# Per-token numbers spread over the partitions by two fp32r products instead of one fp32 product, on one Trainium2 core

## What is computed

```python
def rmsnorm(x, g):
    xf = x.astype(jnp.float32)
    y = xf * lax.rsqrt(jnp.mean(xf * xf, axis=-1, keepdims=True) + EPS)   # one number per token
    return (y * g.astype(jnp.float32)).astype(x.dtype)

# mLSTM, per head and chunk of 128 tokens: a term that depends on the column s alone, ic - b
dmat = b[..., :, None] - b[..., None, :] + ic[..., None, :]
dmat = jnp.where(causal, dmat, -jnp.inf)
m_t = jnp.maximum(inter, dmat.max(axis=-1))
sw = jnp.exp(dmat - m_t[..., None]) * jnp.einsum('bhntk,bhnsk->bhnts', qc, kc)

# odd layer: one softmax over the three dilations, a denominator per token and slot
alpha = jax.nn.softmax(jnp.stack(lses, axis=0), axis=0)
y_c = jnp.einsum('gbsh,gbshe->bshe', alpha.astype(x.dtype), jnp.stack(outs, axis=0))
```

## Time and profile before

| | |
|---|---|
| median of 3 runs | 2983.31 us (2982.22 to 2983.63) |
| the profiled execution's own time | 2986.75 us |
| its span | 2985.0 us |
| mean granted TensorE clock | 0.997 |
| TensorE matmul busy | 2949.0 us, 99% |
| VectorE busy | 1478.3 us, 50% |
| ScalarE busy | 675.4 us, 23% |
| GpSimd busy | 2011.0 us, 67% |
| HBM | 91 GB/s over the span |

### The profile page before, as it was taken

One profiled execution on the slowest core, in us unless ns is written; L12 is line 12 of the kernel. 1 busy time (PEld: TensorE's weight loads), 2 busy tenths in 40 slices (PEclk: granted clock), 3 DMA queues, 4 the chain that ended last, 5 costly groups with the idle time before them and its releaser, 6 DMA issues.

```text
span 2985.0 us, 37813 instructions
## 1 busy us (share of the span) xinstructions
PE 2949.0 (99%) x13898; PEld 2406.9 (81%) x13898; DVE 1478.3 (50%) x2524; ACT 675.4 (23%) x1491; POOL 2011.0 (67%) x2042
## 2 busy tenths in 40 slices
PE   8999999999999999999999999999999999999998
PEld 6887777888888888777888888878888888888887
DVE  7778783633324778775543322565321231424542
ACT  3265353200001346345110000000111111211000
POOL 7775546777777777444777777887776556555775
PEclk9999999999999999999999999999999999999999
DMA  4322222333233322122333333333233223222322
GB/s 147 99 92 65 67 68 77 120 100 97 91 95 127 99 85 93 56 64 62 130 98 92 98 95 103 92 94 100 92 98 106 77 80 105 79 85 78 96 95 77
DMA packets 86921, 274.36 MB, mean 92 GB/s; under 512 B 10368, under 2 KB 11008, under 8 KB 86784
## 3 DMA queue, kind: packets, MB, share of 16 engines
q1 hardware_dynamic: 85248, 270.44, 29.2%
q10 hardware_dynamic: 1536, 2.10, 0.3%
HBM read 266.21 MB, written 4.19 MB: 91 GB/s over the span
## 4 chain that ended last, share of the span: by engine, by line
PE 93%; DVE 5%; POOL 0%; issue 0%; ACT 0%; DMA 0%; DVEq 0%; SPq 0%; POOLq 0%
PE PS L507 59%; PE PS L588 15%; PE PS L858 5%; PE PS L866 3%; PE PS L625 1%; PE PS L904 1%; PE PS L916 1%; PE PS L1155 1%; PE PS L945 1%; PE PS L639 1%; PE PS L928 1%; PE PS L651 1%; DVE SMALLS L1822 0%; PE PS L1130 0%; DVE SQ L1854 0%; PE PS L1142 0%
## 5 line engine op out<-in xcount | busy, mean ns | idle before, releaser
L474 POOL TENSOR_TENSOR WL<-RAW,WH 128x512 fp32r<-128x512 f32 (+2 forms) x538 | 804.2, 1495 | 9.8
L466 POOL TENSOR_TENSOR POOL_C<-POOL_C 128x1 f32<-128x1 f32 x538 | 129.3, 240 | 908.7 <-PE PS L507 518.6
L507 PE MATMUL PS<-XNH,WH 128*128 128x512 f32 (+1 forms) x1712 | 673.7, 394 | 0.7 <-POOL WH L467 0.5
L507 PE MATMUL PS<-XNL,WH 128*128 128x512 f32 (+1 forms) x1712 | 666.9, 390 | 0.0
L471 POOL TENSOR_TENSOR WL<-RAW,WH 128x512 fp32r<-128x512 f32 x420 | 578.9, 1378 | 35.0
L467 POOL TENSOR_SCALAR WH<-RAW 128x1024 fp32r<-128x1024 f32 (+3 forms) x538 | 536.7, 998 | 0.5 <-issue 0.5
L507 PE MATMUL PS<-XNH,WL 128*128 128x512 f32 (+1 forms) x1712 | 423.9, 390 | 0.1
L507 PEld LDWEIGHTS PS<-XNH,WH 128*128 128x128 f32 (+1 forms) x1712 | 320.8, 187 | 70.4 <-issue 3.1
L507 PEld LDWEIGHTS PS<-XNH,WL 128*128 128x128 f32 (+1 forms) x1712 | 320.4, 187 | 68.9 <-POOL WL L474 1.0
L507 PEld LDWEIGHTS PS<-XNL,WH 128*128 128x128 f32 (+1 forms) x1712 | 320.8, 187 | 68.2 <-issue 1.9
L588 PE MATMUL PS<-WH,XNH 128*128 128x512 f32 x704 | 279.1, 396 | 0.2
(11 more groups left out here) (390 smaller groups left out, 4480.1 us busy)
## 6 DMA issues: line engine op xcount, KB each, us to landing
RAW<-w_oslot SPq DMA_DIRECT2D x56, 512.0 KB, 3.6
RAW<-w_L0ffn SPq DMA_DIRECT2D x44, 512.0 KB, 3.6
RAW<-w_L1ffn SPq DMA_DIRECT2D x44, 512.0 KB, 3.6
RAW<-w_od SPq DMA_DIRECT2D x32, 512.0 KB, 3.6
RAW<-w_L0G SPq DMA_DIRECT2D x24, 512.0 KB, 3.6
RAW<-w_L1G SPq DMA_DIRECT2D x24, 512.0 KB, 3.6
RAW<-w_epg SPq DMA_DIRECT2D x16, 512.0 KB, 3.6
RAW<-w_eug SPq DMA_DIRECT2D x16, 512.0 KB, 3.5
```

The costliest lines, as they stand in the source:

```text
L466: nc.gpsimd.tensor_tensor(POOL_C[:, 1:2], POOL_C[:, 0:1], POOL_C[:, 0:1], ALU.add)
L474: nc.gpsimd.tensor_tensor(WL[:, half, at_:w], RAW[:, slot, at_:w], WH[:, half, at_:w].bitcast(F32), ALU.subtract).then_inc(S("weights_spli ...
L507: mm = nc.tensor.matmul(bank, w[:, slot, k * cols:(k + 1) * cols], x[:, k0 + k, :], start=first and j == 0 and w is WH and x is hi, stop=l ...
```

## The change

Every diagonal is made twice: once from the high part of the numbers, rounded to fp32r, and once from the low part, the number less its high part. Both stand in a new buffer SPR (128 x 2 x 512, fp32r), and the parts of the numbers in a new small buffer TINYR. The new function `across` multiplies ones, read as fp32r, by the high and by the low diagonal and lets PSUM add the two. VectorE gets `halve` (two small operations) and `diagonals` (two wide operations, or four of half width at the end). ScalarE writes eight copies a tile instead of four, and TensorE waits for eight. The two new buffers take 4096 + 128 bytes a partition ahead of the shared region, whose end moves with them; WS and BS start at 96 K, INV lies in ARG, and OACC starts at 96 K + 128.

```diff
--- before.py
+++ after.py
@@ -41,7 +41,7 @@
 IN_LAYER = dict(
     conv_raw=8, conv_first=8, conv_acc=8, key_silu=4, mqk_ready=8, v_ready=4, mo_ready=4, small_ready=4, small_staged=1, small_turned=1, sq_raw=4,
     ckvq_raw=4, sk_raw=4, sv_ready=4, dq_raw=4, dk_raw=4, dv_ready=4, nab_ready=1, nab_exp=2,
-    ln_ready=1, lf_ready=1, bg_ready=1, bg_taken=1, diag_ready=16, u_ready=1, den_ready=4, ub_ready=4, ub_taken=4, darg_ready=1,
+    ln_ready=1, lf_ready=1, bg_ready=1, bg_taken=1, diag_ready=32, u_ready=1, den_ready=4, ub_ready=4, ub_taken=4, darg_ready=1,
     pex_ready=17, ms_ready=4, sw_ready=4, kt_ready=3, ktm_copied=3, vw_ready=12, cl_ready=3,
     state_ready=3, swt_ready=4, swt_copied=4, n2_ready=3, n2_taken=3, n1_ready=4, tot_ready=4,
     ya_tm=4, tr_ready=29, tr_copied=29, sq_normed=1, sk_normed=1, dq_normed=1, dk_normed=1,
@@ -186,6 +186,8 @@
         RT = sb(ctx, "RT", [P, T])
         TMP = sb(ctx, "TMP", [P, 2, T])
 
+        SPR = sb(ctx, "SPR", [P, 2, T], F32R)
+        TINYR = sb(ctx, "TINYR", [P, 32], F32R)
         SQA = sb(ctx, "SQA", [P, T])
         small = sb(ctx, "SMALLS", [P, 512])
 
@@ -243,6 +245,9 @@
         TOP8 = tiny(8)
         RTOK = tiny(4)
         RSK = tiny(32)
+        UH, UL = TINYR[:, 0:16], TINYR[:, 16:32]
+        RTH, RTL = UH[:, 0:4], UL[:, 0:4]
+        OSH, OSL = RTH, RTL
         OMX, ONEG, OSUM, OXM = ARG[:, 0:8], ARG[:, 8:16], ARG[:, 16:24], ARG[:, 24:32]
 
         DMS = (DM, X[:, 7, :], SQA[:, :], DG)
@@ -309,7 +314,8 @@
                               skip=16 * K)
         (PLL,) = overlay(("PLL", [P, 2, T], F32R), skip=48 * K)
         GA, ET = SQ, TMP
-        WS, BS, INV = overlay(("WS", [P, 4, P]), ("BS", [P, 4, P]), ("INV", [P, 4, 16]), skip=99840)
+        WS, BS = overlay(("WS", [P, 4, P]), ("BS", [P, 4, P]), skip=96 * K)
+        INV = ARG[:, 0:64].rearrange("p (g t) -> p g t", g=4)
 
         OYH, OYL, OQK = overlay(("OYH", [P, 16, T], F32R), ("OYL", [P, 16, T], F32R), ("OQK", [P, 2, 6, T]))
         OS, OPT = overlay(("OS", [P, NT, T]), ("OPT", [P, NT, T]), skip=16 * K)
@@ -319,7 +325,7 @@
         DIST, SLOPE, BIAS = overlay(("DIST", [P, T]), ("SLOPE", [P, 24]), ("BIAS", [P, T]), skip=92 * K)
         OT = TMP
         ODC, OZ = overlay(("ODC", [P, 2, T]), ("OZ", [P, 2, 6, P]), skip=64 * K)
-        (OACC,) = overlay(("OACC", [P, 2, T]), skip=98 * K + 128)
+        (OACC,) = overlay(("OACC", [P, 2, T]), skip=96 * K + 128)
         OGD = TMP
         (XOUT,) = overlay(("XOUT", [P, KD, T]), skip=64 * K)
         (SQ_FIRST,) = overlay(("SQ_FIRST", [P, KD, T]), skip=68 * K)
@@ -432,7 +438,7 @@
                     sp.dma_start(WS[:, :, :], dram["ws"]).then_inc(S("even_consts"), 16)
                     sp.dma_start(BS[:, :, :].rearrange("p g t -> p (g t)"),
                                  dram["bs"].to_broadcast([P, 4 * P])).then_inc(S("even_consts"), 16)
-                    sp.dma_start(INV[:, :, :].rearrange("p g t -> p (g t)"),
+                    sp.dma_start(ARG[:, 0:64],
                                  dram["inv"].to_broadcast([P, 64])).then_inc(S("even_consts"), 16)
                 if name == "eout":
                     sp.wait_ge(S("x_updated"), 8 * 4)
@@ -609,12 +615,18 @@
                 mm.then_inc(S("tok_summed"), 1)
                 release[bank] = (S("tok_root"), v + 1)
 
+            def across(out_, high, low):
+
+                for x in (high, low):
+                    mm = nc.tensor.matmul(out_, ONES[:, :].bitcast(F32R), x, start=x is high,
+                                          stop=x is low)
+                return mm
+
             def spread_roots(v, bank):
 
                 claim(bank)
                 pe.wait_ge(S("diag_rooted"), v + 1)
-                nc.tensor.matmul(PS[bank][:, :], ONES[:, :], SQ[:, 0, :], start=True, stop=True
-                                 ).then_inc(S("rt_spread"), 1)
+                across(PS[bank][:, :], SPR[:, 0, :], SPR[:, 1, :]).then_inc(S("rt_spread"), 1)
                 release[bank] = (S("rt_ready"), v + 1)
 
             def opening_pair(v, banks, c, sums, roots):
@@ -704,9 +716,8 @@
 
                     b = SPREAD_BANKS[n]
                     claim(b)
-                    pe.wait_ge(*L("diag_ready", 4 * n + 4))
-                    nc.tensor.matmul(PS[b][:, :], ONES[:, :], DG, start=True, stop=True
-                                     ).then_inc(L("ub_ready"), 1)
+                    pe.wait_ge(*L("diag_ready", 8 * n + 8))
+                    across(PS[b][:, :], SPR[:, 0, :], SPR[:, 1, :]).then_inc(L("ub_ready"), 1)
                     release[b] = L("ub_taken", n + 1)
 
                 def in_ckvq(q):
@@ -1159,8 +1170,7 @@
             def spread_sums(s):
 
                 pe.wait_ge(S("o_diag"), s + 1)
-                nc.tensor.matmul(PS[5][:, :], ONES[:, :], SQ[:, 0, :], start=True, stop=True
-                                 ).then_inc(S("o_spread"), 1)
+                across(PS[5][:, :], SPR[:, 0, :], SPR[:, 1, :]).then_inc(S("o_spread"), 1)
 
             def attend_after(s, q):
 
@@ -1258,9 +1268,8 @@
             for half in range(2):
                 cols = slice(256 * half, 256 * half + 256)
                 pe.wait_ge(S("diag_rooted"), 7 + half)
-                nc.tensor.matmul(PS[3][:, cols], ONES[:, :], SQ[:, 0, cols], start=True, stop=True
-                                 ).then_inc(S("rt_spread"), 1)
-            nc.tensor.matmul(PS[2][:, :], ONES[:, :], SQ[:, 0, :], start=True, stop=True).then_inc(S("rt_spread"), 1)
+                across(PS[3][:, cols], SPR[:, 0, cols], SPR[:, 1, cols]).then_inc(S("rt_spread"), 1)
+            across(PS[2][:, :], SPR[:, 0, :], SPR[:, 1, :]).then_inc(S("rt_spread"), 1)
 
 
         @block.scalar
@@ -1401,8 +1410,9 @@
                     if n:
                         act.wait_ge(*L("ub_ready", n))
                     for h in range(M_HEADS):
-                        run(DG[:, h * P:(h + 1) * P], IDENT[:, :], ACT.Copy, L("diag_ready"),
-                            scale=U[:, 4 * n + h:4 * n + h + 1])
+                        for e, of in enumerate((UH, UL)):
+                            run(SPR[:, e, h * P:(h + 1) * P], IDENT[:, :], ACT.Copy, L("diag_ready"),
+                                scale=of[:, 4 * n + h:4 * n + h + 1].bitcast(F32))
 
                 act.wait_ge(*L("u_ready", 1))
                 diagonal(0)
@@ -1732,21 +1742,30 @@
                 V.tensor_tensor(SQA[:, :], SQA[:, :], SQ[:, k % 2, :] if v else SQ_FIRST[:, k, :], ALU.add
                                 ).then_inc(S("sq_added"), 1)
 
+            def halve(of, high, low):
+
+                then(V.tensor_scalar(high, of, 1.0, 0.0, ALU.mult, ALU.add))
+                then(V.tensor_tensor(low, of, high.bitcast(F32), ALU.subtract))
+
+            def diagonals(high, low, n0, n):
+
+                for e, of in enumerate((high, low)):
+                    ins = V.tensor_tensor(heads(SPR[:, e, n0 * P:(n0 + n) * P], n),
+                                          IDENT[:, :].unsqueeze(1).to_broadcast([P, n, P]),
+                                          of[:, n0:n0 + n].bitcast(F32).unsqueeze(2).to_broadcast([P, n, P]), ALU.mult)
+                return ins
+
             def roots(v):
 
                 dve.wait_ge(S("tok_root"), v + 1)
                 then(V.reciprocal(RTOK, RTOK))
+                halve(RTOK, RTH, RTL)
                 if v == 6:
                     for half in range(2):
-                        V.tensor_tensor(heads(SQ[:, 0, 256 * half:256 * half + 256], 2),
-                                        IDENT[:, :].unsqueeze(1).to_broadcast([P, 2, P]),
-                                        RTOK[:, 2 * half:2 * half + 2].unsqueeze(2).to_broadcast([P, 2, P]), ALU.mult
-                                        ).then_inc(S("diag_rooted"), 1)
+                        diagonals(RTH, RTL, 2 * half, 2).then_inc(S("diag_rooted"), 1)
                     dve.wait_ge(S("rt_spread"), 8)
                     return
-                V.tensor_tensor(heads(SQ[:, 0, :], NT), IDENT[:, :].unsqueeze(1).to_broadcast([P, NT, P]),
-                                RTOK.unsqueeze(2).to_broadcast([P, NT, P]), ALU.mult
-                                ).then_inc(S("diag_rooted"), 1)
+                diagonals(RTH, RTL, 0, NT).then_inc(S("diag_rooted"), 1)
                 dve.wait_ge(S("rt_ready"), v + 1)
 
             def add_residual(update, banks, c0, per, scaled=False):
@@ -1951,8 +1970,10 @@
                 dve.wait_ge(*L("bg_taken", 1))
                 B, G = BG[:, 0:16], BG[:, 16:32]
                 V.memset(MPREV[:, 0:4], M_INIT)
-                V.tensor_tensor(U.rearrange("p (n c) -> p n c", n=NT), i_pre,
-                                B.rearrange("p (n c) -> p n c", n=NT), ALU.subtract).then_inc(L("u_ready"), 1)
+                then(V.tensor_tensor(U.rearrange("p (n c) -> p n c", n=NT), i_pre,
+                                     B.rearrange("p (n c) -> p n c", n=NT), ALU.subtract))
```

(7 more changed lines are left out.)

## The result

After the change the median is 2994.49 us (7 runs, 2992.83 to 2995.07) against 2983.31 for the kernel before (7 runs). The ratio is 1.0035 with a 95% interval from 1.0025 to 1.0044: slower by 11.2 us by the medians, where 6 us less were forecast and the range ended at 2981.5. The profiled execution took 2995.07 us, 8.3 more than its like of before.

The account below looks back on a forecast made before the run. PE's own queue was taken to set the time nearly everywhere. The terms 0.42 + 3.5 + 3.3 - 0.95 - 0.14 gave 6.1 us saved, the median going from 2983.31 to 2977.2 us, range 2975.2 to 2981.5.

Parts of the forecast that it names:

- Memory: Buffer placement: 4224 bytes more ahead of the shared region, no live buffer overlaid; cost nothing, bounds a microsecond either way.
- the change doesn't do what it says: Rival: a product read as fp32r through a bitcast still runs as fp32; 2986.5 us or far more, chance 0.02.
- mLSTM products, 8: PE's mLSTM spreads: six save 0.45 us each, two save 0.41 each, together 3.5 us.
- sums, 8: PE's spreads of the attention sums: 8 x 0.41 = 3.3 us saved; the fp32 transposes before them stay.
- first root: First per-token root spread on PE, with some 4 us from reciprocal to spread: saves 0.4 us.
- five roots behind an opening pair: Root spreads where PE must wait for DVE's second diagonal: 0.19 us net cost each, five times 0.95.
- the end: Kernel's last root, half diagonals feeding DVE's last products: cost 0.14 us, between 0 and 0.74.
- The roots: Five roots behind opening pairs: PE starts 1.97 us after the reciprocal, waits 0.50, restart 0.11 more, 0.42 back.
- Diagonals of ACT and DVE hidden: ACT's eight mLSTM copies (about 2.5 us) and DVE's extra work for the attention sums fit in idle time: cost nothing.
- GpSimd in the way at the roots: Rival: GpSimd stretches the second diagonal at five roots, 5 x 0.77 us more, 2.2 saved, 2981.1; chance 0.06.
- The layers keep nothing: Rival: DVE's run to 265 is tied to its own work, 3.9 us saved become waits; 2981.1 us, chance 0.10.
- The clock falls behind the new waits: Rival: waits at five roots drop TensorE's clock, 1.7 us each, 8.5 us lost; 2985.7 us, chance 0.03.

Follow-up runs that it names:

- b_memory: Kernel before with only the change's memory part, SPR and TINYR allocated but unused, shared region at 126720: 2998.72 us, ratio 1.0052.
- a_pad128: Whole change with 128 bytes more in front of the shared region, which starts at 126848: 2978.87 us, ratio 0.998 to the kernel before.
- a_late_again: Against a_pad128, root products of the five opening pairs four low-weight matmuls later: 2976.33 us, ratio 0.997 to the kernel before.
- a_root_k2: Against a_late_again, root products one matmul earlier: 2973.46 us, ratio 0.9964 to the kernel before.

## Why the prediction was wrong

The step that failed is *Memory*: "a multiple of 128, and no buffer is laid over another that was live ... Cost nothing, bounds a microsecond either way." I asked what lies over what and what is loaded when, and never what address an operand starts at. `b_memory` has that part alone and loses 13.7 us. No row of before could price it, since all fp32r operands there had the same remainder of 256; that the trace is silent on it was the reason to bound it wider than a microsecond, or to make it a rival. The rival that the change doesn't do what it says looked at fp32r only.

The rest can be read against `a_pad128`, which is the change without that step: 6.2 us saved (0.998) where 6.1 were forecast, and 5.5 in its second measurement. By the starts of the same matmuls in the traces of before and `a_pad128`:

| term | forecast | measured |
|---|---|---|
| mLSTM products, 8 | -3.5 | -3.5 (six at 0.45, two at 0.39 and 0.42) |
| sums, 8 | -3.3 | -3.5 (0.44 each, the first 0.41) |
| first root | -0.4 | -0.4 |
| five roots behind an opening pair | +0.95 | +1.4 (0.29 each, one 0.22) |
| the end | +0.14 | +0.07, from the reciprocal to DVE's last products |
| together | -6.1 | -5.9 |

The two traces differ by 8.2 us in all. The rest is no part of the change: `a_pad128` has one fall of the clock before the end where the kernel before has two, and one of the two waits for DVE of 1.39 us is short in it.

- *Products at 0.45 us:* right. The sums gained 0.03 each more than said, but for the first: the turn from the fp32 transposes to fp32r is shared out differently, I counted none of it.
- *The roots:* the mechanism was right and the size a little off. PE starts 2.05 us behind the reciprocal and not 1.97, so the product is 0.60 us late by its own place in the stream. The profile shows 0.43 of it as a wait, since it counts the matmul before as busy until its result is out. 0.60 + 0.08 for the restart less 0.42 is 0.26; ten matmuls further on the starts are 0.29 late.
- *Diagonals of ACT and DVE hidden:* right. In the odd layer the two operations took 3.38 us, not 1.5 to 2.9, with GpSimd beside them, and were still ready before PE came:

```profile
2316.75 0.89 DVE L1747 TENSOR_SCALAR TINYR<-SMALLS 128x4 fp32r<-128x4 f32 x1
2317.67 0.16 DVE L1748 TENSOR_TENSOR TINYR<-SMALLS,TINYR 128x4 fp32r<-128x4 f32 x1
2317.87 3.38 DVE L1753 TENSOR_TENSOR SPR<-IDENT,TINYR 128x512 fp32r<-128x512 f32 x2
2321.28 0.69 DVE L2415 TENSOR_TENSOR OQK<-PS,RT 128x512 f32<-128x512 f32 x1
2322.55 0.69 DVE L2419 SCALAR_TENSOR_TENSOR OQK<-PS,RT 128x512 f32<-128x512 f32 x1 [0.58 <-PE PS L513]
```

- *GpSimd in the way at the roots:* it wasn't, because it came too late: the two diagonals took 1.29 us together at the second root, to 589.54, and GpSimd's split of the next chunk began at 589.56, behind one small instruction at 589.40. It is so at all five roots, so the question which of the two would wait wasn't put there.
- *The layers keep nothing:* fell. The wait at the transposes is 3.1 us twice, as in the earlier trace rows, and what was saved before it stayed saved.
- *The range:* its lower end isn't what the prediction says it is. The lower bounds of the root and end terms, -2.1 us for the roots and 0 for the end, give 9.3 us saved and 2974.0, not 2975.2, and the parts of "within" add up to 0.51 and not 0.50. Neither had a share in the miss.
- *The clock falls behind the new waits:* it didn't at any of the five roots behind an opening pair. But the price that I put on a fall, 1.7 us, is of the size that decides between runs: `a_late_again` and `a_root_k2` differ by 1.4 us for their clocks between 263 and 274 us.

## What to carry to other kernels

An edit that adds a buffer is also an edit of every address behind it. Before it is priced at nothing, list the start of both operands of the matmuls that bound the kernel: here a distance that was a multiple of 256 bytes gave 0.2267 us for 512 columns, one of 128 or 32 gave 0.2333, and 2208 such matmuls ate more than twice what 22 better products saved. And when a chain of four small steps is made longer by one wide operation, look for a place further down the bound engine's queue: at four of five roots a place four matmuls later gave back 0.69 us, more than the wait of 0.43 itself, and at the fifth, where the result was wanted soon, it cost 0.27 to 0.29.

## What the runs showed that I had not expected

- The pace of fp32r matmuls of 512 columns depends on the distance of the two operands' starts within a partition: 0.2267 us at multiples of 256 bytes (0 or 256 modulo 512, both were run), 0.2333 at 128, 0.2289 at 64, 0.2333 at 32. Moving both together changes nothing. At 128 it holds with the weights as the stationary side and as the moving one; at 64 the 96 matmuls with weights moving lost three times as much as those with weights stationary. What makes it so is not shown; the slow pace is there with no other engine and no DMA at work.
- Busy share and waits give no sign of it. The mean duration of a group does, if shapes and operands are kept apart: 389 ns goes to 397 (groups of instructions by line, before and after; busy us, mean ns, idle). A long stretch of the chain divided by its count, or the starts of the same matmul in two traces, gives the size.

```profile
L507 PE MATMUL PS<-HH,WH 128*128 128x512 f32 x352 | 136.9, 389 | 0.0
```

```profile
L513 PE MATMUL PS<-HH,WH 128*128 128x512 f32 x352 | 139.6, 397 | 0.0
```

- One operation of DVE beside GpSimd, 0.29 or 1.43 us long, decides over a wait of PE of 0.24 or 1.39 us. Two such places make up to 2.3 us between traces of kernels that are alike there.
- The same 3.1 us wait of PE is followed by a lower clock in some profiles and not in others:

```profile
262.00:267.00 5.00, 1.97 (x16) 1.72 (x15) 4.90 (x7) 2.03 (x5) 1.37 (x1) 0.95 0.20 57
267.00:271.00 4.00, 4.00 (x22) 3.03 (x21) 2.92 (x6) 2.76 (x8) 0.00 (x0) 0.64 0.00 0
```

  These are the stretches of the kernel before, 0.95 and 0.64, against 1.00 and 1.00 in `a_root_k2` above. The Trainium skill, TensorE: Matmul & The Clock Gate, section What's actually happening, has the gate watch the engine without regard to when the kernel started, so that the point of change varies; the rows agree with that in so far as the clock differs behind the same wait.
